# Gate products of the recurrence inside the next weight block, recurrence ahead of the next convolution, mixing blocks in order gate, gate, value, value

## The reference, cut to what matters

```python
h = rms_norm(x, g_mix_pre)
u_pool, x_rnn, g_rnn, gate_p, gate_r = split(h @ w_in)     # 512, 1024, 1024, 1024, 1024
# recurrent branch, per 128 features ("chunk"), 8 chunks
xc = causal_dwconv(x_rnn, conv_w, conv_b)                  # 4 taps
r, i = sigmoid(xc @ w_gates[0] + b0), sigmoid(xc @ w_gates[1] + b1)
a = exp(-8 * r * softplus(-lambda))
mult = sqrt(1 - a * a), but 1 at the first token
hid[t] = a[t] * hid[t-1] + mult[t] * i[t] * xc[t]          # the scan
y_rnn = hid * gelu(g_rnn)
# pooling branch, 4 groups of 128 features
y_pool[g] = ((mean of the last 2, 4, 8 or 16 tokens) - u_pool) @ pool_w[g] * pool_scale
merged = sigmoid(gate_r) * (y_rnn @ w_rg_out) + sigmoid(gate_p) * (y_pool @ w_pool_out)
x = x + rms_norm(merged @ w_o, g_mix_post)                 # then a feed-forward part
```

## Time and profile before

| what | us |
|---|---|
| median of 3 runs | 3427.11 |
| lowest, highest | 3426.26, 3429.72 |
| the profiled execution | 3436.78 |
| its span in the profile | 3434.9 |
| TensorE busy in it | 3126.4 (91%) |
| VectorE, ScalarE, POOL busy | 1507.7, 799.2, 1148.0 |
| mean granted TensorE clock | 0.953 |

### The profile page before, as it was taken

How to read it: one execution, slowest core, us unless ns; L and a number is a source line. 1 busy time by engine, 2 the same in 40 slices (tenths; PEclk the granted TensorE clock), 3 DMA queues, 4 the chain that set the end, 5 groups by cost and what they waited for, 6 DMA issues and landing times.

```text
span 3434.9 us, 40717 instructions
## 1 busy us (share of the span) xinstructions
PE 3126.4 (91%) x17024; PEld 2523.1 (73%) x17024; DVE 1507.7 (44%) x1585; ACT 799.2 (23%) x1008; POOL 1148.0 (33%) x525
## 2 busy tenths in 40 slices
PE   6998998998789898899698899999699999999869
PEld 5877876777677787787376688778388888888647
DVE  3134328339723424634766601323743044244366
ACT  1111225112211123411344401121311011011241
POOL 2232220135433231044033344343144344444323
PEclk9999999999889999999799999999899999999989
DMA  5200111332131011121111111112111111111211
GB/s 229 68 31 13 39 34 48 141 135 67 56 123 35 13 45 43 45 83 70 67 39 35 35 46 53 37 55 92 61 49 49 49 49 49 47 45 49 79 44 73
DMA packets 59237, 208.06 MB, mean 61 GB/s; under 512 B 5856, under 2 KB 7648, under 8 KB 59104
## 3 DMA queue, kind: packets, MB, share of 16 engines
q1 hardware_dynamic: 42240, 143.15, 12.4%
q10 hardware_dynamic: 16864, 62.97, 4.9%
HBM read 188.27 MB, written 17.83 MB: 60 GB/s over the span
## 4 chain that ended last, share of the span: by engine, by line
issue 41%; PE 32%; POOL 14%; DVE 9%; DMA 3%; ACT 1%; POOLq 0%; ACTq 0%; SPq 0%; DVEq 0%
PE ps L529 23%; POOL w_hi L463 8%; POOL w_lo L465 6%; DVE Sb L1622 3%; PE ps L783 2%; DMA raw<-s 1%; PE ps L695 1%; DMA modfirst<-modw 1%; PE ps L556 1%; DVE stage L1713 1%; DVE ST L1565 1%; PE ps L612 1%; DVE stage L1728 1%; PE ps L804 1%; DVE Y L1708 1%
## 5 line engine op out<-in xcount | busy, mean ns | idle before, releaser
L463 POOL TENSOR_TENSOR w_hi<-raw,pool_zero 128x1024 fp32r<-128x1024 f32 (+1 forms) x242 | 454.2, 1877 | 2181.7 <-PE ps L529 2159.8
L465 POOL TENSOR_TENSOR w_lo<-raw,w_hi 128x1024 fp32r<-128x1024 f32 (+1 forms) x242 | 658.7, 2722 | 19.0
L529 PE MATMUL ps<-g_hi,w_hi 128*128 128x512 f32 x1600 | 502.8, 396 | 37.7 <-DVE g_lo L1448 36.0
L529 PE MATMUL ps<-h_hi,w_hi 128*128 128x512 f32 (+1 forms) x1832 | 498.0, 368 | 43.0 <-ACT QK L1000 13.9
L529 PE MATMUL ps<-g_lo,w_hi 128*128 128x512 f32 x1600 | 495.1, 391 | 0.0
L529 PE MATMUL ps<-g_hi,w_lo 128*128 128x512 f32 x1600 | 494.4, 390 | 0.0
L529 PE MATMUL ps<-h_lo,w_hi 128*128 128x512 f32 (+1 forms) x1832 | 475.5, 355 | 0.0
L529 PE MATMUL ps<-h_hi,w_lo 128*128 128x512 f32 (+1 forms) x1832 | 474.5, 355 | 0.0
L529 PEld LDWEIGHTS ps<-h_hi,w_hi 128*128 128x128 f32 x1832 | 305.8, 191 | 117.0 <-issue 47.9
L529 PEld LDWEIGHTS ps<-g_hi,w_hi 128*128 128x128 f32 x1600 | 301.6, 189 | 111.8 <-issue 39.4
L529 PEld LDWEIGHTS ps<-g_lo,w_hi 128*128 128x128 f32 x1600 | 302.2, 189 | 63.5
(11 more groups left out here) (293 smaller groups left out, 3329.0 us busy)
## 6 DMA issues: line engine op xcount, KB each, us to landing
...
modfirst<-modw SPq DMA_DIRECT2D x4, 1024.0 KB, 10.8
...
```

What stands on the lines that cost most here:

```text
L463: G.tensor_tensor(w_hi[s][:, :n], raw[s][:, :n], zero.to_broadcast([P, n]), ALU.add).then_inc(hi_done, 1)
L465: G.tensor_tensor(w_lo[s][:, :n], raw[s][:, :n], w_hi[s][:, :n].bitcast(F32), ALU.subtract)\
L529: last = T.matmul(ps[:, o + c0:o + c0 + size], wt[s][:, kk], xx[:, k, t0:t0 + size], start=(x == 0 and n == 0), stop=(x == k_n - 1 and n = ...
```

## The change

1. The gate products of chunk c are issued inside block 2c+2, behind its k step 3 (the fourth of eight); those of chunk 7 inside the first block of the first mixing.
2. VectorE does `recurred(c)` before `convolved(c + 1)`.
3. Both mixings run gate, gate, value, value for two planes at a time; SP's and POOL's loops take the weights in that order, four blocks a turn. ScalarE's r_hi of chunk 7 comes behind its first mixing evacuation.
4. The pooling product of group c is issued inside the next block behind its k step 6, the last one inside the first block of the second mixing. ScalarE scales and copies a pooling product before it evacuates the next block.
5. Planes 0 to 5 of the merged result are split behind the last two gate evacuations of the second mixing, ahead of its last two values.

No operation is added or removed. The core of the diff:

```diff
-            return [(g, (at_[i + 1] - g) // 2, (s8, place(g), 2), (s8, place(g) + 1, 2), KD, KD)
+            return [(g, (at_[i + 1] - g) // 2, [(s8, place(g) + x, 2, KD) for x in range(2)])
                     for i, g in enumerate(at_[:-1])] + [
-                (G_PMIX, 8, (s8, S8_GP, 1), (s4, 0, 1), KD, 4),
-                (G_WO, 40, (s8, S8_WO, 2), (s8, S8_WO + 1, 2), KD, KD),
-                (G_PLEP, 4, (s2, 0, 2), (s2, 1, 2), 2, 2),
-                (G_PLEG, 4, (s8, S8_PLEG, 2), (s8, S8_PLEG + 1, 2), KD, KD)]
+                (G_RMIX, 4, [(s8, place(G_RMIX) + x, 4, KD) for x in (0, 2, 1, 3)]),
+                (G_POOL, 2, [(s8, place(G_POOL) + x, 2, KD) for x in range(2)]),
+                (G_PMIX, 4, [(s8, S8_GP, 2, KD), (s8, S8_GP + 1, 2, KD), (s4, 0, 2, 4), (s4, 1, 2, 4)]),
...
-            for g0, pairs, a0, a1, k0, k1 in runs(BIAS_CUTS):
+            for g0, turns, places in runs(BIAS_CUTS):
                 if g0 in BIAS_CUTS[1:3]:
                     biases(BIAS_CUTS.index(g0) - 1)
                 lo = 1 if g0 == 0 else 0
-                with sp.Fori(lo, pairs) as j:
-                    for s, (array, place, step), k in ((0, a0, k0), (1, a1, k1)):
-
-                        sp.wait_ge(split_done, j * 2 + (g0 + s - 1))
-                        load(None, s, array, j * step + place, k)
+                with sp.Fori(lo, turns) as j:
+                    for x, (array, place, step, k) in enumerate(places):
+
+                        sp.wait_ge(split_done, j * len(places) + (g0 + x - 1))
+                        load(None, x % 2, array, j * step + place, k)
...
+            def rnn_gate_maps(c):
+
+                def maps(k):
+                    if k != 3:
+                        return
+                    pe.wait_ge(tab_in, 112)
+                    pe.wait_ge(rnn_xc, c + 1)
+                    if c:
+                        pe.wait_ge(rnn_act, c)
+                    for m in range(2):
+                        for t0, c0, size in SEC:
+                            last = T.matmul(ps[:, (4 + 2 * m) * BANK + c0:(4 + 2 * m) * BANK + c0 + size],
+                                            rgwt[:, 8 * m + c, :], xcs[c % 2][:, t0:t0 + size], start=True, stop=True)
+                    last.then_inc(rnn_gates, 1)
+
+                return maps
+
             for c in range(8):
-                slab(G_RNN + 2 * c, 0, g_hi, g_lo, KD, SEC, 2, SPLITS["h2"] if c == 0 else None)
+                slab(G_RNN + 2 * c, 0, g_hi, g_lo, KD, SEC, 2, SPLITS["h2"] if c == 0 else None,
+                     between=rnn_gate_maps(c - 1) if c else None)
                 slab(G_RNN + 2 * c + 1, 1, g_hi, g_lo, KD, SEC, 2)
-                pe.wait_ge(tab_in, 112)
-                pe.wait_ge(rnn_xc, c + 1)
-                if c:
-                    pe.wait_ge(rnn_act, c)
-                for m in range(2):
+            for j in range(4):
+                slab(G_RMIX + 4 * j, 0, g_hi, g_lo, KD, SEC, 2, between=rnn_gate_maps(7) if j == 0 else None)
+                slab(G_RMIX + 4 * j + 1, 1, g_hi, g_lo, KD, SEC, 2)
+                slab(G_RMIX + 4 * j + 2, 0, r_hi, r_lo, KD, SEC, 2, SPLITS["rnn"] if j == 0 else None)
+                slab(G_RMIX + 4 * j + 3, 1, r_hi, r_lo, KD, SEC, 2)
+
+            def pool_map(c):
+
+                def maps(k):
+                    if k != 6:
+                        return
+                    pe.wait_ge(pool_d, c + 1)
+                    if c:
+
+                        pe.wait_ge(sp_hi, SPLITS["pool"] + c)
                     for t0, c0, size in SEC:
-                        last = T.matmul(ps[:, (4 + 2 * m) * BANK + c0:(4 + 2 * m) * BANK + c0 + size],
-                                        rgwt[:, 8 * m + c, :], xcs[c % 2][:, t0:t0 + size], start=True, stop=True)
-                last.then_inc(rnn_gates, 1)
-            for k in range(KD):
-                slab(G_RMIX + 2 * k, 0, g_hi, g_lo, KD, SEC, 2)
-                slab(G_RMIX + 2 * k + 1, 1, r_hi, r_lo, KD, SEC, 2, SPLITS["rnn"] if k == 0 else None)
-
-            for c in range(5):
-                if c < 4:
-                    slab(G_POOL + c, c % 2, g_hi, g_lo, KD, SEC, 2)
-                if c:
-                    pe.wait_ge(pool_d, c)
-                    if c > 1:
-
-                        pe.wait_ge(sp_hi, SPLITS["pool"] + c - 1)
-                    for t0, c0, size in SEC:
-                        last = T.matmul(ps[:, 4 * BANK + c0:4 * BANK + c0 + size], C2[:, 15, (c - 1) * P:c * P],
+                        last = T.matmul(ps[:, 4 * BANK + c0:4 * BANK + c0 + size], C2[:, 15, c * P:(c + 1) * P],
                                         C2[:, 12, t0:t0 + size], start=True, stop=True)
                     last.then_inc(pool_ps, 1)
-            for k in range(KD):
-                slab(G_PMIX + 2 * k, 0, g_hi, g_lo, KD, SEC, 2)
-                slab(G_PMIX + 2 * k + 1, 1, r_hi, r_lo, 4, SEC, 2, SPLITS["pool"] if k == 0 else None)
+
+                return maps
+
+            for c in range(4):
+                slab(G_POOL + c, c % 2, g_hi, g_lo, KD, SEC, 2, between=pool_map(c - 1) if c else None)
+            for j in range(4):
+                slab(G_PMIX + 4 * j, 0, g_hi, g_lo, KD, SEC, 2, between=pool_map(3) if j == 0 else None)
+                slab(G_PMIX + 4 * j + 1, 1, g_hi, g_lo, KD, SEC, 2)
+                slab(G_PMIX + 4 * j + 2, 0, r_hi, r_lo, 4, SEC, 2, SPLITS["pool"] if j == 0 else None)
+                slab(G_PMIX + 4 * j + 3, 1, r_hi, r_lo, 4, SEC, 2)
...
-            rnn_high(7)
-
-            def mix(g0, first):
-                for n in range(KD):
-                    if n + first >= 2:
-                        act.wait_ge(mix_used, first + n - 1)
-                    evac(g0 + 2 * n, T2[:, n % 2, :], SEQ, 2, ACT.Sigmoid)
-                    evac(g0 + 2 * n + 1, T2[:, 2 + n % 2, :], SEQ, 2)
-
-            mix(G_RMIX, 0)
+
+            def mix_gate(g0, first, n):
+
+                if n + first >= 2:
+                    act.wait_ge(mix_used, first + n - 1)
+                evac(g0 + 4 * (n // 2) + n % 2, T2[:, n % 2, :], SEQ, 2, ACT.Sigmoid)
+
+            def mix_value(g0, n):
+
+                evac(g0 + 4 * (n // 2) + 2 + n % 2, T2[:, 2 + n % 2, :], SEQ, 2)
+
+            for j in range(4):
+                mix_gate(G_RMIX, 0, 2 * j)
+                if j == 0:
+                    rnn_high(7)
+                mix_gate(G_RMIX, 0, 2 * j + 1)
+                mix_value(G_RMIX, 2 * j)
+                mix_value(G_RMIX, 2 * j + 1)
...
+            def merged_highs(k0, k1):
+
+                for k in range(k0, k1):
+                    act.wait_ge(mix_used, 8 + k + 1)
+                    A.activation(g_hi[:, k, :], B2[:, k, :], ACT.Copy).then_inc(sp_hi, 1)
+
+            for j in range(4):
+                mix_gate(G_PMIX, 8, 2 * j)
+                mix_gate(G_PMIX, 8, 2 * j + 1)
+                if j == 3:
+                    merged_highs(0, 6)
+                mix_value(G_PMIX, 2 * j)
+                mix_value(G_PMIX, 2 * j + 1)
+            merged_highs(6, KD)
...
                 gated_input(c)
+                recurred(c)
                 if c < 7:
                     convolved(c + 1)
-                recurred(c)
             for n in range(KD):
-                dve.wait_ge(evac_done, G_RMIX + 2 * n + 2)
+                dve.wait_ge(evac_done, G_RMIX + 4 * (n // 2) + n % 2 + 3)
                 V.tensor_tensor(B2[:, n, :], T2[:, n % 2, :], T2[:, 2 + n % 2, :], ALU.mult).then_inc(mix_used, 1)
...
+            def merged_low(k):
+
+                dve.wait_ge(sp_hi, SPLITS["merged"] + k + 1)
+                V.tensor_tensor(g_lo[:, k, :], B2[:, k, :], g_hi[:, k, :].bitcast(F32), ALU.subtract).then_inc(sp_lo, 1)
+
             for n in range(KD):
-                dve.wait_ge(evac_done, G_PMIX + 2 * n + 2)
+                if n == 6:
+                    for k in range(6):
+                        merged_low(k)
+                dve.wait_ge(evac_done, G_PMIX + 4 * (n // 2) + n % 2 + 3)
```

More of the change, by code:

```diff
@@ L483, in weighted_queries @@
                         last.then_inc(qw_ready, 1)
-            for g0, pairs, a0, a1, k0, k1 in runs(CUTS):
+            for g0, turns, places in runs(CUTS):
                 if g0 == 0:
@@ L490, in _ @@
                 lo = 1 if g0 == 0 else 0
-                with pool.Fori(lo, pairs) as j:
-                    for s, k in ((0, k0), (1, k1)):
-                        g = j * 2 + (g0 + s)
-                        pool.wait_ge(raw_loaded[s], j * 16 + (8 * g0 + 16))
+                with pool.Fori(lo, turns) as j:
+                    for x, (_, _, _, k) in enumerate(places):
+                        g = j * len(places) + (g0 + x)
+                        pool.wait_ge(raw_loaded[x % 2], j * (8 * len(places)) + (8 * (g0 + x - x % 2) + 16))
                         pool.wait_ge(slab_done, g - 1)
-                        split(s, k, g)
-                if g0 + 2 * pairs in CUTS[1:3]:
-                    weighted_queries(CUTS.index(g0 + 2 * pairs) - 1)
```

(24 more changed lines are left out.)

11 lines of the change are left out of this document (5 added, 6 removed).

## The result

| | before | after |
|---|---|---|
| median of 11 runs each, us | 3430.86 | 3441.51 |
| lowest, highest | 3426.26, 3436.27 | 3435.56, 3444.29 |
| the profiled execution | 3436.78 | 3444.29 |
| its span | 3434.9 | 3442.5 |
| mean granted TensorE clock | 0.953 | 0.953 |

The changed kernel is slower: ratio 1.0027, 95% interval 1.0019 to 1.0035, which is 9.3 us of 3430.86. The two medians themselves differ by 10.65 us (1.0031), inside that interval. In the two profiled executions the recurrence lost 20.7 us, and pooling and the start of the output projection gave back 12.1.

The account below looks back on a forecast made before the run. The recurrence's pace was taken as set by a ring through VectorE and ScalarE, lengthened by lowered clock and POOL blocking. 22.1 - 8.0 - 4.8 = +9.3 us, added to 3427.11, gave 3436.4; range 3421 to 3443.

Parts of the forecast that it names:

- products to W: Recurrence, gate products' start to POOL's next w_hi: 12.00 us behind a stall, against 9.13 at full clock.
- ring: Recurrence, one chunk's gate products to the next's, through VectorE and ScalarE: 34.19 us, where chunks took 29.9 before.
- stall: TensorE's wait ahead of the gate products in each ring of the new order: 5.95 us.
- Part 1: Gate products half a block later and recurrence before the next convolution: a cost of 22.1 us, bounds 14.5 and 24.0.
- Part 3: Pooling products inside the next block: a gain of 8.0 us, bounds 7 to 9.1, with 1.1 of wait left.
- Part 4: Six of eight merged planes split before the last values: a gain of 4.8 us, bounds 0 to 10.3.
- check on chunk 7: End of the recurrence: r_lo ready some 21 us after chunk 7's products, its reader at 25.8, so that wait goes.
- Part 2: Both mixings in order gate, gate, value, value: no gain or loss; a full split fits beside a value block by 0.2.
- The first: Rival, recurrence: stalls inside a block cost only what the 4.02 stalls do (10.92); +1.7 us, 3428.8; chance 0.22.
- the second: Rival, recurrence: the clock isn't lowered in a stall in mid-block; -10.8 us, 3416.3; chance 0.10.
- The third: Rival, second mixing: doubly blocked splits overrun the value block by 0.9, four times; +3.6 on the forecast, 3440; chance 0.08.
- The fourth: Rival, recurrence: VectorE and POOL don't block each other, ring 25.3 us; 53 faster, 3374; chance 0.02.

Follow-up runs that it names:

- e7: The changed kernel with POOL's two split operations for the sixteen recurrence blocks cut from 1024 to 64 columns each; 3384.77 us, ratio 0.9860 to before.
- e4: The changed kernel with 24 unused TensorE products ahead of the wait of the gate products of chunks 1 to 7; 3423.60 us, ratio 0.9980 to before.
- e3: The changed kernel with the recurrence wholly as before (products between blocks, convolution ahead of the recurrence); 3417.49 us, ratio 0.9962 to before.

## Why the prediction was right

W is again the start of POOL's w_hi at the end of the block that holds the gate products.

| step | predicted | measured |
|---|---|---|
| root's start after W | 6.35 | 6.34 |
| scan's start after W | 8.90 | 8.89 |
| r_lo's end after W | 17.30 | 17.29 |
| next products after W | 22.19 | 22.08 |
| products to W | 12.00 | 12.03 (11.53 in the first stalled ring) |
| ring | 34.19 | 33.97 (last six) |
| stall | 5.95 | 5.85 |
| cost of Part 1 | 22.1 | 20.7 |
| gain of Part 3 | 8.0 | 7.8 |
| gain of Part 4 | 4.8 | 4.3 |
| second mixing | 0 | 0.6 lost |
| sum | +9.3 | +9.2 |

The rows from W are read at W = 1907.56: the root at 1913.90, the scan at 1916.45, r_lo's end at 1922.64 + 2.21, the products at 1929.64.

That the sum agrees to 0.1 is luck: Part 1 costs 1.4 less than was forecast, Parts 3 and 4 gain 0.7 less and the second mixing loses 0.6, and these cancel. What is not luck is that each term is right to within 1.4.

The forecast in absolute time was 3436.4, and 3441.51 was measured. Of these 5.1 us, 3.75 are the kernel before: three runs had put it at 3427.11, eleven put it at 3430.86. The forecast range ended at 3443, 6.6 above the forecast, so the base taken from three runs used up more than half of that room.

**Part 1.** The ring was built from pieces of the old trace in which the same operations met POOL's splits, and every piece held. The offsets were not the same. L1852 started 0.96 behind w_hi's start in the piece and L1892 starts 0.27 behind it here, and w_hi was asked for 1.15 after the scan's start there and 1.98 after it here, so that it takes 2.00 and not 2.83. Yet the ends agree (the root at W + 6.34, the scan's start to r_lo's end 8.40 in both), since each blocked operation ends a fixed time after the one that it waits for: 1.09 and 1.08 after w_hi's end.

The 1.4 us between 22.1 and 20.7 is ring length: the last six average 33.97 where 34.19 was worked out, 6 x 0.22 = 1.3 (the first, 31.21, was worked out as 31.32). It comes from the first of the six, 33.6, and from a tenth in the convolution's part of each. By the Trainium skill, "SBUF — State Buffer", section "SBUF: two separate sides", a held lock stops the other engine for the whole instruction; here w_hi ends at 1909.45 and L1892 at 1910.53, 1.08 after it where it takes 1.23 alone, so the overlap that the prediction kept from the rows (0.14) is there again (0.15). e7 shows the blocking as cause, e4 the clock.

The prediction's check on chunk 7 counted too short: its r_lo is ready 29.4 after its products (1990.94 + 2.22 - 1963.74), as the prediction's own 12.00 + 17.30 says, and not 21. The reader comes later too, at 32.5 (1986.74 + 7 x 1.36 - 1963.74), so that no wait stands there all the same.

**Part 2.** Almost right. The full split beside a half-depth value block was said to fit by 0.2, and it does: the split that begins at 2217.99 ends at 2223.22, the block at 2223.43. But the block that reads it takes 11.16 to 11.20 us and not 10.88, in each of three turns, and TensorE's weight loads idle 0.3 for w_lo in it (from 2256.3 to 2267.4). The second mixing takes 120.3 against 119.7, a loss of 0.6 where the prediction had nothing. And e3 shows that the order saves 4.6 when the recurrence is the old one, 2.7 of waiting for r_lo and the slower blocks behind it, which the prediction did not credit to it by name.

**Part 3.** From 2187.80 to 2201.73 are 13.93, and one product of 1.77 is now in the block before. The wait is 0.98, where 1.1 was taken.

**Part 4.** The stall is 3.59 (3.7 predicted), and blocking has its part in it: six lows (the g_lo of six planes) take 12.81 beside POOL's splits where six alone would take 6.9. That the stall would go without it was not tested. The size is right partly by luck. The prediction's terms (2.1 + 8.1 + 4.8 + 8.6, less four overlaps of 0.14) add up to 23.0 and not to its 22.7; measured are 22.9 from the last gate block's end at 2311.27. TensorE stops 19.4 after that end where 19.0 was taken, and the two slips cancel. From 2322.06 to 2338.92 are 16.86 against 21.19; the gain is 4.3 and not 4.8 because 2.4 us, and not 1.8, come on top of the block and the stall.

**Rivals.** The first (12.00 would be 10.92) and the second (no low clock in mid-block) fall with 12.03 and a granted clock of 0.50 to 0.53. The third happened at about a sixth of its size, 0.6 of 3.6, and not as it was told: in three of the four turns only w_lo is blocked in the split beside the value block. In the last turn w_hi takes 2.15 as well, and the first output block waits 0.17 for w_lo. The fourth is what e7 makes by force, at 25.3 a ring as worked out.

**The span.** It differs by 7.6, not 9.2. The recurrence started 1.9 earlier in the changed kernel's profiled execution, in code that the change does not touch; 0.3 more came behind. The ratio over eleven runs of each, 1.0027 or +9.3, agrees with the sum; the medians, 10.65 apart, do so less well. That this difference ahead of the recurrence is chance, and not the change, is argued from its spread over the kernels run (1686.2 to 1699.5), not shown.
